# Slot lists of two experts in one product of 128 weight columns and four moving columns, read back by halves of the partitions

## The reference, cut to what matters

```
scores = sigmoid(xf @ w_router);  biased = scores + b_router
_, idx = top_k(where(expert_mask, biased, NEG_INF), 8)      # 8 experts for each of 256 tokens
w = take_along_axis(scores, idx);  w = w / sum(w) * 2.5
# each expert e gets the tokens that chose it, in slots; out = swiglu(x[toks], w1[e], w3[e], w2[e]) * weight
routed = segment_sum(y, slot_tok);  shared = swiglu(xf, ws1, ws3, ws2)
return routed + shared
```

## Time and profile before

| | |
|---|---|
| device time, median of 3 runs | 2778.12 us (2777.23 to 2779.72) |
| profiled execution, its own time | 2778.27 us |
| its span | 2777.0 us |
| PE busy | 2625.8 us, 95% of the span |
| DVE busy | 814.0 us, 29% |
| DMA | 658.65 MB, mean 237 GB/s |
| L1679, the lists' products | 528 instructions |
| L1848 and L1849, reading them | 66 instructions each |
| the experts of the two layers, from the first up product to the last | 438 to 965 us and 1387 to 1917 us |

### The profile page before, as it was taken

The page is one execution under the profiler, slowest core; times in us unless marked ns, Lnnn a source line. Parts: engine busy times, 40 slices in busy tenths (PEclk is TensorE's granted clock), DMA queues, the critical chain, the costliest instruction groups (busy, mean ns, idle before and its releaser), DMA issues.

```text
span 2777.0 us, 29138 instructions
## 1 busy us (share of the span) xinstructions
PE 2625.8 (95%) x11563; PEld 1530.6 (55%) x11563; DVE 814.0 (29%) x2126; ACT 536.7 (19%) x1141; POOL 168.6 (6%) x202
## 2 busy tenths in 40 slices
PE   8998999999999899979999999978999999999987
PEld 5765884343343366658834334333346667765664
DVE  0584122232221127512323222121231232211274
ACT  2225111000010021330101001001321222121254
POOL 3000000000000000000001000000000000001110
PEclk9999999999999999999999999998999999999999
DMA  9758656999999923475589999997005201101300
GB/s 343 245 212 323 244 231 247 403 414 405 415 417 411 386 92 130 163 257 202 230 334 393 408 406 417 419 418 271 15 0 182 71 21 61 61 8 66 146 1 16
DMA packets 176691, 658.65 MB, mean 237 GB/s; under 512 B 17777, under 2 KB 47769, under 8 KB 125216
## 3 DMA queue, kind: packets, MB, share of 16 engines
q1 hardware_dynamic: 163376, 634.32, 58.6%
q0 software_dynamic: 12736, 22.32, 2.3%
q10 hardware_dynamic: 432, 0.01, 0.0%
HBM read 670.45 MB, written 3.51 MB: 243 GB/s over the span
## 4 chain that ended last, share of the span: by engine, by line
PE 87%; DMA 4%; DVE 3%; ACT 3%; issue 1%; SPq 1%; POOL 0%; DVEq 0%; ACTq 0%
PE ps L231 38%; PE ps L1725 16%; PE ps L1775 8%; PE ps L1761 8%; PE ps L1401 2%; DMA ring<-in_w 2%; PE ps L2325 2%; PE ps L1706 2%; DMA ring<-in_w_mod 2%; PE ps L527 2%; PE ps L888 1%; PE ps L2817 1%; PE ps L1740 1%; PE ps L808 1%; PE ps L1679 1%
## 5 line engine op out<-in xcount | busy, mean ns | idle before, releaser
L231 PE MATMUL ps<-hT,ring 128*128 128x256 f32 (+2 forms) x2480 | 647.4, 420 | 14.9 <-DMA ring<-in_w_in 10.6
L231 PEld LDWEIGHTS ps<-hT,ring 128*128 128x128 f32 (+1 forms) x2480 | 468.4, 190 | 193.5 <-issue 121.2
L1725 PE MATMUL ps<-ring,ar 128*64 128x512 f32 x1984 | 442.1, 599 | 31.7 <-DMA ring<-in_w 29.5
L1725 PEld LDWEIGHTS ps<-ring,ar 128*64 128x64 f32 x1984 | 146.2, 138 | 318.3 <-issue 318.3
L1775 PE MATMUL ps<-ar 128*128 128x512 f32 x528 | 244.2, 605 | 0.0
L1761 PE MATMUL ps<-ring,ar 128*64 128x512 f32 x1008 | 233.8, 599 | 0.0
L231 PE MATMUL ps<-ar,ring 128*128 128x256 f32 (+1 forms) x672 | 210.6, 471 | 4.7 <-ACT ar L2605 2.3
L231 PEld LDWEIGHTS ps<-ar,ring 128*128 128x128 f32 x672 | 158.8, 237 | 53.3 <-issue 14.8
L1775 PEld LDWEIGHTS ps<-ar 128*128 128x128 f32 x528 | 94.9, 189 | 148.2 <-issue 147.8
L1952 DVE TENSOR_TENSOR ar<-ar,ps 128x256 f32<-128x256 f32 x66 | 27.8, 421 | 476.0 <-ACT ar L1821 476.0
L231 PE MATMUL ps<-ring,hT 128*128 128x256 f32 (+1 forms) x640 | 156.5, 402 | 0.0
(11 more groups left out here) (395 smaller groups left out, 2368.4 us busy)
## 6 DMA issues: line engine op xcount, KB each, us to landing
ring<-in_w SPq DMA_DIRECT2D x374, 1024.0 KB, 10.4
ring<-in_w_mod SPq DMA_DIRECT2D x36, 2048.0 KB, 14.0
ring<-in_w_in SPq DMA_DIRECT2D x16, 2048.0 KB, 15.1
ring<-in_ab_w_in SPq DMA_DIRECT2D x28, 1024.0 KB, 11.0
ring<-in_w_in SPq DMA_DIRECT2D x6, 4096.0 KB, 13.5
ar<-in_w SPq DMA_DIRECT2D x20, 1024.0 KB, 12.8
ring<-in_w_out SPq DMA_DIRECT2D x4, 2048.0 KB, 16.0
ring<-in_ab_w_out SPq DMA_DIRECT2D x2, 4096.0 KB, 13.9
```

The lines of the kernel that those rows point to most:

```text
L231: ins = te.matmul(o, l, r, start=(first and i == 0), stop=(last and i == len(pairs) - 1), skip_group_check=lax)
L1725: ins = te.matmul(b[BOTH[u], :], K.x_b[:, kk, BOTH[u]], w[u][:, :, kk, :], start=(kk == 0), stop=(kk == 7))
```

## The change

The products of `pe_slots` and of `pe_beyond` no longer run once for each expert. One product for each half of the tokens takes all 128 columns of the 0/1 matrix as weights and four moving columns: token number and weight of expert 0, token number and weight of expert 1. So there are two products a pair, four instructions in the trace, with 128 weight columns. The result has four PSUM columns on all partitions, of which partitions 0 to 63 need the first two and partitions 64 to 127 the last two; the others hold what belongs to no slot. `slot_rows` therefore reads by halves of the partitions: two copies and two additions of 64 partitions in place of one copy and one addition of 128. `K.more_tok_w` swaps two of its axes so that the four columns lie together; `choose` has as many operations as before.

```diff
@@ pe_first_slots
     for p in range(2):
-        ins = yield from pe_slots(K, l, p, b, 2 * p)
+        ins = yield from pe_slots(K, l, p, b, 4 * p)
@@ pe_slots
     te.wait_ge(*(yield ("select", l, p)))
-    for u in range(2):
-        for i in range(2):
-            r = K.tok_w[:, i, 2 * p + u, :] if p < PAIRS else K.more_tok_w[:, u, i, :]
-            ins = te.matmul(b[BOTH[u], at:at + 2], s[:, i, BOTH[u]], r, start=(i == 0), stop=(i == 1))
-    K.ps["slot_ps", l, p] = b[:, at:at + 2]
+    for i in range(2):
+        r = K.tok_w[:, i, 2 * p:2 * p + 2, :] if p < PAIRS else K.more_tok_w[:, i, :, :]
+        ins = te.matmul(b[:, at:at + 4], s[:, i, :], r.rearrange("p u c -> p (u c)"), start=(i == 0), stop=(i == 1))
+    K.ps["slot_ps", l, p] = b[:, at:at + 4]
     return ins
@@ slot_rows
-    K.ve.tensor_copy(K.slot[:, p, :], ps).then_inc(*dve())
-    return K.ve.tensor_scalar(K.slot_row[:, p:p + 1], ps[:, 0:1], NO_TOKEN, None, ALU.add).then_inc(*dve())
+    for u in range(2):
+        n = BOTH[u]
+        K.ve.tensor_copy(K.slot[n, p, :], ps[n, 2 * u:2 * u + 2]).then_inc(*dve())
+        K.ve.tensor_scalar(K.slot_row[n, p:p + 1], ps[n, 2 * u:2 * u + 1], NO_TOKEN, None, ALU.add).then_inc(*dve())
@@ choose
-        ve.tensor_copy(K.more_tok_w[:, b, :, 0], C(K, "token")).then_inc(*dve())
+        ve.tensor_copy(K.more_tok_w[:, :, b, 0], C(K, "token")).then_inc(*dve())
...
-            dst = at[:, b, :] if a == 0 else K.more_tok_w[:, b, :, 1]
+            dst = at[:, b, :] if a == 0 else K.more_tok_w[:, :, b, 1]
```

More of the change, by code:

```diff
@@ L2043, in pe_beyond @@
     te.wait_ge(*(yield ("b_select", l, x)))
-    for u in range(2):
-        for i in range(2):
-            ins = te.matmul(g0[BOTH[u], 0:2], s[:, i, BOTH[u]], K.more_tok_w[:, u, i, :], start=(i == 0), stop=(i == 1))
+    for i in range(2):
+        ins = te.matmul(g0[:, 0:4], s[:, i, :], K.more_tok_w[:, i, :, :].rearrange("p u c -> p (u c)"), start=(i == 0),
+                        stop=(i == 1))
     ins.then_inc(*pe("b_slot_ps", l, x))
@@ L2099, in dve_beyond @@
     ve.wait_ge(*(yield ("b_slot_ps", l, x)))
-    slot_rows(K, dve, PAIRS, g0[:, 0:2])
+    slot_rows(K, dve, PAIRS, g0[:, 0:4])
     dve.also("b_slot", l, x)
```

## The result

Over 20 runs of each kernel on one chip the changed kernel takes 2783.91 us (2777.77 to 2790.66) and the one before 2778.32 us (2772.84 to 2785.27). The ratio is 1.0021 with a 95% interval of 1.0013 to 1.0030: 5.6 us slower, 3.6 to 8.3. The forecast was 2777.1 with a range to 2781.0; the time lies above it, on the side that the rival "slower, by DVE's reads" describes. The profiled execution of the changed kernel had 2789.58 us, near the top of its runs, so its trace is used for durations and waits and not for the total.

The account below looks back on a forecast made before the run. PE and the weight stream were taken as both full, nearly in step. PE's terms, passed through the stream, gave -1.1 us in layer 0 and -0.1 in layer 1: -1.2 from 2778.27, so 2777.1 us; range 2773.8 to 2781.0.

Parts of the forecast that it names:

- slower, by DVE's reads: Rival: four reads in a row at 0.15 us delay PE, a full stream returns nothing; 2781.2 us, chance 0.10.
- PE, the lists of a turn: Scatter to down products: four list instructions take 0.45 us, not 0.55; 0.10 us less per turn, -3.0 us a layer.
- by the loads: Rival: four moving columns cost 0.24 us each, so lists take 0.41 us more a turn; 2806 us, chance 0.02.
- by the count of instructions: Rival: each list instruction costs 0.043 us whatever its width, gaining 0.38 us a turn; 2769.8 us, chance 0.05.
- PE, the first lists: Lists of pairs 0 and 1: sixteen instructions become eight at 0.112 us; +0.1 us a layer, bounds 0 to +0.2.
- DVE, reading by halves: DVE reads of the list results: two more instructions cost +0.30 us a pair, bounds +0.13 to +0.47.
- Who pays: Ordinary pairs hide the longer DVE reads; pairs 4, 6, 7, 8 and 9 pay in full, +1.5 us a layer.
- From PE to the end: How PE's 1.4 us shorter layer reaches the end through the weight stream: -1.1 us in layer 0, -0.1 in layer 1.
- the dents: Windows where the weight stream isn't full, letting PE's gain pass: 1.5 us in layer 0, 1.0 in layer 1.
- pair 30's turn: The turn of pair 30, whose weights PE waits for: its own gain of 0.1 us a layer counts at the end.
- nothing passes: Rival: the weight stream is full throughout, so only pair 30's turn counts, 2 x 0.1; 2778.1 us, chance 0.15.
- The clock: PE restarts at 1.2 GHz behind the weights' wait; may move a layer's end some tenths either way, left in the range.

Follow-up runs that it names:

- before_p69_wait: The kernel before with eight more one-column DVE copies in each of pairs 6 to 9 of each layer: +5.6 us, ratio 1.0020.
- before_p4_wait: The kernel before with seven more one-column DVE copies in pair 4 of each layer only: +1.4 us, ratio 1.0005.
- after_again: The changed kernel unaltered, timed again against the kernel before: +4.4 us, ratio 1.0016, at equal clock +1.2 us.
- products_only: The changed kernel with the old reads over all 128 partitions, against the kernel before: -2.8 us, ratio 0.9990.
- after_fixed_reversed: The changed kernel with upper half read first, listing's first piece a pair earlier, pieces of pairs 5 to 9 behind L1939's copy; against the kernel before: -6.1 us, ratio 0.9978.

## Why the prediction was wrong, step by step

**PE, the lists of a turn: right in the sum, in part by luck.** Scatter to down is 5.16 us where 5.18 was forecast, and no step stands ahead of the lists. But the four take 0.36 us and not 0.45, since the first one's load is covered and only the others are 0.11 apart; and against a turn without lists (4.73) 0.07 us are left behind them, where the forecast had both steps go. The two errors cancel. The rivals "by the loads" and "by the count of instructions" are out.

**PE, the first lists: right.** From the start of the last product ahead of them to the first product behind L1692 it is 4.89 us in both layers, and was 4.78: +0.11, with +0.1 forecast.

**DVE, reading by halves: the first step that failed.** Its price was put at +0.30 us with +0.47 as the upper end, and it is +0.50. The +0.30 came from two holds of 0.09; there are three, of 0.10 to 0.13. The upper end assumed that only the four reads could stand in each other's way; the copy behind them was held too. The two added instructions are 0.15 us, and three stops of 0.10 to 0.13 make the rest. The Trainium skill ("VectorE: DVE Perf Modes", section "Two Vector instructions with no wait between them") compares an input in PSUM with the last instruction that read PSUM, however many others stand between. By it L1939, which starts at partition 0, is held after a last read from partition 64, and is free when the halves are swapped. The trace agrees: 0.77 us against 0.65. I had applied the rule to the reads and their follower only, and left out the next reader of PSUM, which was the one that PE waits for.

**Who pays: right as to place.** Ordinary pairs hide it; pairs 4 and 6 to 9 don't. Pair 4 pays only 0.38 us (a wait of 2.04 against 1.66), because the third stop stands at L1939, behind what its products wait for; the others pay the 0.50, so 2.4 us a layer. before_p69_wait and before_p4_wait show each part alone.

**From PE to the end: right in kind, with the wrong input and too large a return.** The prediction's own working at 0.50 us gives, after pair 9, 0.1 - 0.9 + 2.5 = +1.7 us. In layer 0 that is +1.5 at pair 11, and less 1.5 for the dents and 0.1 for pair 30's turn -0.1; in layer 1, less 0.7 by pair 16 and 0.1, it is +0.9. Together +0.8 us (+0.6 with pair 4 at 0.38), where after_again at equal clock shows +1.2 ± 1.2, or up to +2.9 if the 5 us above are not credited. That a gain on PE turns into a longer wait at pair 30 is seen in products_only and after_fixed_reversed. But the dents returned less than the 1.5 us that layer 0 was given. Against the stage's start, the trace of products_only is 1.1 us ahead at pair 10 and still 1.1 ahead behind the wait, so nothing that PE won after pair 10 passed; the changed kernel is 1.4 us late at pair 10 and 0.8 behind the wait, so 0.6 came back. In layer 0 the rival "nothing passes" fits these two traces better than the forecast. Layer 1 can't settle it: its wait scatters between 14.0 and 16.6 us in the kernels without joined products, and the kernel before has the longest.

**The clock: the second step that failed, a term not priced.** The prediction left "some tenths" for it. The changed kernel had 10 us more at the lower level in after_again, 3.5 us of its +4.4 by the slope. In its trace 4.7 us more of that level than in the kernel before lie in the two waits for weights, where PE has nothing to do; if they cost nothing, 1.9 us are left (my estimate, 0.35 x 5.3). So the clock took 2 to 3.5 us. What brings it is only half settled. Counting layers of all profiles, the clock fell right behind pair 4 in 10 of 14 with a wait of 2.04 us or more, and in 1 of 14 with 1.66 us or less; so the longer wait there matters for that stretch. But before_p4_wait has the wait and no lower mean clock, and products_only, without it, may have 5.7 us more at the lower level, within its error of none. The kernels with joined products all lie above zero in the last column, but so does reads_only, which has none (11.6). Part of it is the longer wait for weights. Whether the joined products lower the clock anywhere else stays open, as does how much of the difference in mean clock is chance: the two measured +5.6 and +4.4 hold it, and no kernel here takes it away alone.

**The rivals.** "Slower, by DVE's reads" is what happened: reads at nearly their full length, paid for in five pairs, and a stream that doesn't give it back. It had a chance of 0.10, and its own deciding point was 0.18 us of DVE a pair, below the value that I had chosen. The forecast nevertheless held the gain as the likeliest, since it let the stream's dents return it. But by the price left without the clock, +1.2 to +2.9 us, the kernel would have stood at 2779.5 to 2781.2, inside the forecast's range (to 2781.0) or at its edge; it is the clock on top that carries it out. So the faults are of different kinds: 0.20 us too little in a term that is paid eight times, and 0.08 too little in pair 4 of each layer, 1.8 us in all, a return by the stream that was put up to 1.5 us too high in layer 0, and a term of 2 to 3.5 us that had no place in the sum.

## What to carry to other kernels

When DVE work is split by partitions, price each change of the start partition at about 0.12 us as measured here, and look past the split instructions to the next one that reads PSUM; then ask in which stages other work on DVE has used up the cover, since only there it is paid. Saving on PE in a stage where the DMA engines are full bought here mostly a longer wait for the next weights. Work that nobody waits for soon, here the listing's pieces, belongs behind the copy that TensorE needs: that reordering was worth more than the edit (-4.7 us, ratio 0.9983, 0.9974 to 0.9993).

## What the runs showed of the hardware that was not expected

- A DVE instruction with nothing to wait for (L1939) started 0.12 us later (0.77 against 0.65 us behind the selection's start) when the last instruction that had read PSUM, five places ahead, read it from the other half of the partitions.
- Runs of one kernel differ by up to 14 us, and most of it goes with the mean granted clock: 0.35 us for each us at the lower level, correlation 0.83. Taking it out cut the standard error of a comparison from about 1.1 to about 0.6 us.
- Part of a difference in mean clock can cost nothing. The mean was 0.9791 over the 20 runs of the changed kernel and between 0.9809 and 0.9817 for the kernel before on three chips; in the profiled executions of the two, the changed kernel had 5.7 us more at the lower level in the two waits for pair 30's weights, in which PE was idle.
